# A four-layer network plus one block on one core: where the normed activations start in SBUF

## The reference

```
for i in range(4):                                   # mixers: retention, RG-LRU, MLA, retention
    h = layer_norm(ALPHA * h + mixer(h), ...)
    h = layer_norm(ALPHA * h + square(relu(h @ w1)) @ w2, ...)      # D_FF 4096
x = h + 0.5 * swiglu(rmsnorm(h), ...)                # D_FF 2816
x = x + hybrid_mixer(rmsnorm(x), ...)                # dilated attention + grouped-query attention, gated
x = x + 0.5 * swiglu(rmsnorm(x), ...)
return rmsnorm(x)
```

## The kernel before

| tensor | bytes after a slot's start, modulo 256 | used as |
|---|---|---|
| `ht_hi`, `ht_lo` | 64 | moving in U, stationary in T |
| `mlp_hi`, `mlp_lo` | 0 | stationary in D |
| `ffn_hi`, `ffn_lo` | 192 | stationary in D |
| `ry` (retention rows) | 64 | stationary in D |
| `lu` | 192 | stationary in D, moving in 60 U |
| `mo` of heads 0 to 3, of heads 4 to 7 | 160, 64 | stationary in D |
| `mrg` | 96 | stationary in D |
| `oa`, `ob`, `m_chi`, `m_clo` | 64 | moving in U |

## Time and profile before

### The profile page before, as it was taken

How to read it: one execution, slowest core, us unless ns; L and a number is a source line. 1 busy time by engine, 2 the same in 40 slices (tenths; PEclk the granted TensorE clock), 3 DMA queues, 4 the chain that set the end, 5 groups by cost and what they waited for, 6 DMA issues and landing times.

```text
span 2217.1 us, 31071 instructions
## 1 busy us (share of the span) xinstructions
PE 2089.2 (94%) x13232; PEld 1848.0 (83%) x13232; DVE 1284.3 (58%) x1205; ACT 924.5 (42%) x866; POOL 191.4 (9%) x76
## 2 busy tenths in 40 slices
PE   8999999978999879999999999989989999699998
PEld 7887899876998657998988799879978878687997
DVE  6756655687555635656656655564454556444544
ACT  5344333365333433333335433343344445444433
POOL 0001000121000113001000200010010003311000
PEclk9999999989999999999999999999999999999999
DMA  8443555434554404554544455525547543243552
GB/s 309 153 172 132 209 189 189 157 114 152 190 189 166 156 21 171 189 189 152 209 152 162 154 207 187 191 87 202 195 152 231 145 136 115 76 152 124 186 208 98
DMA packets 32366, 364.23 MB, mean 164 GB/s; under 512 B 3677, under 2 KB 3938, under 8 KB 10130
## 3 DMA queue, kind: packets, MB, share of 16 engines
q1 hardware_dynamic: 28146, 347.49, 42.6%
q0 software_dynamic: 4128, 15.39, 2.6%
HBM read 361.77 MB, written 1.10 MB: 164 GB/s over the span
## 4 chain that ended last, share of the span: by engine, by line
PE 84%; DVE 11%; ACT 3%; issue 1%; DMA 0%; SPq 0%; DVEq 0%; ACTq 0%
PE acc L860 25%; PE bank L820 15%; PE bank L822 14%; PE bank L821 14%; PE bank L847 2%; PE bank L849 2%; PE bank L848 2%; DVE h L2151 2%; PE bank L813 1%; PE bank L1372 1%; PE bank L1020 1%; PE bank L930 1%; PE bank L1408 1%; DVE w_lo L2078 1%; DVE h L2138 1%
## 5 line engine op out<-in xcount | busy, mean ns | idle before, releaser
L820 PE MATMUL bank<-ht_hi,w_hi 128*128 128x256 f32 x2720 | 764.8, 281 | 7.5 <-DVE ob_lo L2661 6.6
L822 PE MATMUL bank<-ht_hi,w_lo 128*128 128x256 f32 x2720 | 761.0, 280 | 0.0
L821 PE MATMUL bank<-ht_lo,w_hi 128*128 128x256 f32 x2720 | 760.2, 279 | 0.0
L820 PEld LDWEIGHTS bank<-ht_hi,w_hi 128*128 128x128 f32 x2720 | 511.4, 188 | 14.8 <-issue 12.7
L821 PEld LDWEIGHTS bank<-ht_lo,w_hi 128*128 128x128 f32 x2720 | 511.4, 188 | 2.5 <-issue 0.5
L822 PEld LDWEIGHTS bank<-ht_hi,w_lo 128*128 128x128 f32 x2720 | 512.5, 188 | 0.0
L2078 DVE TENSOR_TENSOR w_lo<-raw,w_hi 128x4096 fp32r<-128x4096 f32 (+3 forms) x87 | 328.0, 3770 | 142.7 <-ACT w_hi L1525 142.7
L1513 ACT ACTIVATE w_hi<-raw 128x2048 fp32r<-128x2048 f32 x174 | 323.4, 1908 | 143.4 <-PE bank L822 138.6
L1525 ACT ACTIVATE w_hi<-raw 128x4096 fp32r<-128x4096 f32 (+3 forms) x87 | 269.2, 3094 | 188.4 <-PE bank L822 188.4
L2073 DVE TENSOR_TENSOR w_lo<-raw,w_hi 128x2048 fp32r<-128x2048 f32 x98 | 220.2, 2288 | 113.3 <-ACT w_hi L1513 113.2
L789 POOL TENSOR_TENSOR w_lo<-raw,w_hi 128x2048 fp32r<-128x2048 f32 x18 | 82.4, 4579 | 1597.5 <-ACT w_hi L1513 1597.5
(11 more groups left out here) (321 smaller groups left out, 2726.0 us busy)
## 6 DMA issues: line engine op xcount, KB each, us to landing
raw<-slabs_in SPq DMA_DIRECT2D x147, 2048.0 KB, 7.7
raw<-slabs_in SPq DMA_DIRECT2D x23, 1024.0 KB, 6.3
raw<-slabs_in SPq DMA_DIRECT2D x12, 512.0 KB, 9.6
g_tab<-gains_in POOLq DMA_DIRECT2D x11, 512.0 KB, 6.7
a_bias<-bias_rows POOLq DMA_DIRECT2D x8, 576.0 KB, 6.9
b_tab<-gains_in POOLq DMA_DIRECT2D x8, 512.0 KB, 7.8
raw<-slabs_in SPq DMA_DIRECT2D x2, 1152.0 KB, 5.6
raw<-slabs_in SPq DMA_DIRECT2D x1, 1280.0 KB, 7.2
```

Source lines behind the costliest of these rows:

```text
L820: nc.tensor.matmul(o, whi, xhi, start=first, stop=False)
L821: nc.tensor.matmul(o, whi, xlo, start=False, stop=False)
L822: return nc.tensor.matmul(o, wlo, xhi, start=False, stop=last)
```

## The change

`ht_hi` and `ht_lo` get buffers that are 256 bytes longer. Inside them, each stage uses a view that begins `a` bytes in, with its own `a` for hi and for lo. The buffers themselves now begin at distance 0 from the slots, and `off_w` behind them is 256 bytes, so that everything behind moves by 512 bytes and keeps its distance modulo 256. `a` is thus the distance that the table above gives as 64 before:

| stage n | kind | `ht_hi`, `ht_lo` now | U of `ht` | T of `ht` |
|---|---|---|---|---|
| 0 | retention | 128, 128 | 768 | 192 |
| 1 | MLP | 128, 128 | 768 | |
| 2 | RG-LRU | 192, 192 | 480 | |
| 3 | MLP | 192, 192 | 768 | |
| 4 | MLA | 0, 0 | | 48, and 48 with 192 columns |
| 5 | MLP | 32, 32 | 768 | |
| 6 | retention | 64, 64 | 768 | 192 |
| 7 | MLP | 96, 96 | 768 | |
| 8 | FFN | 64, 192 | 1056 | |
| 9 | hybrid | 128, 0 | 960 | 288 |
| 10 | FFN | 160, 160 | 1056 | |

The three passes of U run in the order hi x hi, hi weights x lo activations, lo weights x hi activations; in stage 6 the last two change places.

```diff
+HT_PLACE = [(128, 128), (128, 128), (192, 192), (192, 192), (0, 0), (32, 32), (64, 64), (96, 96), (64, 192), (128, 0), (160, 160)]
+PASS_ORDER = [('whh', 'whl', 'wlh'), ('whh', 'whl', 'wlh'), ('whh', 'whl', 'wlh'), ('whh', 'whl', 'wlh'), ('whh', 'whl', 'wlh'), ('whh', 'whl', 'wlh'), ('whh', 'wlh', 'whl'), ('whh', 'whl', 'wlh'), ('whh', 'whl', 'wlh'), ('whh', 'whl', 'wlh'), ('whh', 'whl', 'wlh')]
...
-        off_w(64)
-        ht_hi = sb("ht_hi", [P, KD, S], F32R)
-        ht_lo = sb("ht_lo", [P, KD, S], F32R)
-        off_w(192)
+        ht_hi_buf = sb("ht_hi", [P, KD * S + 64], F32R)
+        ht_lo_buf = sb("ht_lo", [P, KD * S + 64], F32R)
+        ht_hi_at = [ht_hi_buf[:, a // 4:a // 4 + KD * S].rearrange("p (k s) -> p k s", k=KD) for a, _ in HT_PLACE]
+        ht_lo_at = [ht_lo_buf[:, a // 4:a // 4 + KD * S].rearrange("p (k s) -> p k s", k=KD) for _, a in HT_PLACE]
+        off_w(256)
...
-                nc.tensor.matmul(o, whi, xhi, start=first, stop=False)
-                nc.tensor.matmul(o, whi, xlo, start=False, stop=False)
-                return nc.tensor.matmul(o, wlo, xhi, start=False, stop=last)
+                passes = {"whh": (whi, xhi), "whl": (whi, xlo), "wlh": (wlo, xhi)}
+                for i, name in enumerate(order):
+                    w, x = passes[name]
+                    m = nc.tensor.matmul(o, w, x, start=first and i == 0, stop=last and i == 2)
+                return m
...
             for layer in range(DEPTH):
+                use_ht(2 * layer)
                 (retention, lru, mla)[layer % 3](layer)
+                use_ht(2 * layer + 1)
                 mlp(layer)
+            use_ht(N_LN)
             ffn(0)
+            use_ht(N_LN + 1)
             hybrid()
+            use_ht(N_LN + 2)
             ffn(1)
```

More of the change, by code:

```diff
@@ L799, in _, with use_ht @@
         def _(pe):
-            down_count = [0]
+            ht_hi, ht_lo, order = ht_hi_at[0], ht_lo_at[0], PASS_ORDER[0]
+            def use_ht(n):
+                nonlocal ht_hi, ht_lo, order
+                ht_hi, ht_lo, order = ht_hi_at[n], ht_lo_at[n], PASS_ORDER[n]
             def wait_free(*key):
@@ L1554, in ht_parts @@
                         act.wait_ge(*full(*key))
-                        nc.scalar.activation(ht_hi[:, 4 * half:4 * half + 4, t * P:(t + 1) * P],
+                        nc.scalar.activation(ht_hi_at[n][:, 4 * half:4 * half + 4, t * P:(t + 1) * P],
                                              psum(*key)[:, :].rearrange("p (c q) -> p c q", c=4), ACT.Copy)\
@@ L2098, in ht_part @@
                 dve.wait_ge(ht_hi_ready, 4 * n + 2 * t + half + 1)
-                nc.vector.tensor_tensor(ht_lo[:, c, q], psum(*key)[:, :].rearrange("p (c q) -> p c q", c=4),
-                                        ht_hi[:, c, q].bitcast(F32), ALU.subtract).then_inc(read_sem(*key), 1)
+                nc.vector.tensor_tensor(ht_lo_at[n][:, c, q], psum(*key)[:, :].rearrange("p (c q) -> p c q", c=4),
+                                        ht_hi_at[n][:, c, q].bitcast(F32), ALU.subtract).then_inc(read_sem(*key), 1)
             def ht_parts(n, tiles=range(TT)):
```

## The result

| | before | changed |
|---|---|---|
| median of 18 runs, us | 2220.97 | 2225.45 |
| ratio, 95% interval | | 1.0023 (1.0016 to 1.0029) |
| span of the profiled execution, us | 2217.1 | 2222.8 |

The account below looks back on a forecast made before the run. PE bounds the kernel, through the pitch of its U matmuls. From 2218.9 us, U adds 12.1 and T takes 0.6, swapped passes and other engines 0: 2230 us, stated median 2231; range 2199 to 2255, 8 in 10.

Parts of the forecast that it names:

- What bounds the kernel: PE, 84% of the chain of waits; U's 117.8 ns pitch goes into the time in full, clock unchanged.
- That the distance matters: D and T pitches differ by up to 6.6 ns with the stationary-minus-moving distance: good around 0, bad from 64 to 160.
- The second rival: Nothing changes: D's spread has another cause and U stays at 117.8 ns; 2219 to 2223 us, chance 15%.
- D's differences carried over to U at half size: U's change per matmul is (D(s - m) - 229.2) / 2, from -0.85 to +2.45 ns by stage; sum +12.1 us.
- sign of being wrong: For U: the prediction is wrong if places 96 to 192 are not slower than 64.
- the two distances without a row: D's unmeasured distances: 128 got its neighbours' mean, 233.9 ns; 224, between 192 and 0, got 228.4.
- the range from 2199 to 2255: Total time, us: holds the forecast, second rival, half the first and most of the third; 8 in 10.
- T and D by distance: T takes D's pitch at its new distance, stage 4 falling to 227.5 ns; T sum -0.6 us, D groups unchanged.
- The swapped passes: Stage 6: each pass reads at the same distance in either order, so 0 us; U stays at 117.8 ns.
- The first rival: U's fast 113.3 ns rhythm takes over: gain 16 us if half the changed stages, 30 if all; chance 27%.
- The third rival: A slower U rhythm: one 4.4 ns step gives +25 us, 2244 to 2247; chance 15%, 4 for over 2%.

Follow-up runs that it names:

- All-0: Changed kernel with ht_hi and ht_lo at place 0 in all 11 stages, passes in the old order: 2229.82 us, 1.0042 of before.
- all-224: Changed kernel with ht_hi and ht_lo at place 224 in all 11 stages, passes in the old order: 2226.66 us, 1.0028 of before.
- all-192: Changed kernel with ht_hi and ht_lo at place 192 in all 11 stages, passes in the old order: 2201.20 us, 0.9915 of before.

## Why the prediction was right, and which steps were not

**What bounds the kernel: right.** The pitch went into the time. By the pitches read, U should have added 4.9 us (below) and T taken 0.5; the span grew by 5.7, so about 1.3 us lie between the groups and are not assigned. The clock stayed, 0.977 against 0.978.

**That the distance matters: right.** All-0, all-224 and all-192 have the same instructions and differ by up to 28.6 us, while the shift by 96 bytes with equal distances is worth 0.06%, with an interval that holds no change. The second rival is refuted, and so is what the prediction drew from the Trainium skill, page "TensorE: Matmul & The Clock Gate", section "Step-by-step: what each phase is for": that the change would be worth nothing. Whether it is the two read ports that meet, no run shows.

**D's differences carried over to U at half size: the step that failed.** The prediction named a sign of being wrong that came true: U at place 192 was not slower than at 64, but faster (stage 2) or equal (stage 3). The rule gave the right sign of the total because it was near at 128 and 96, the places of three stages.

| stage, place | forecast ns | measured ns | us forecast | us measured |
|---|---|---|---|---|
| 0, 128 | 120.1 | 118.7 and 120.0 | +1.8 | +1.2 |
| 1, 128 | 120.1 | 120.0 (first 192: 118.7) | +1.8 | +1.5 |
| 2, 192 | 119.8 | 113.3 | +1.0 | -2.1 |
| 3, 192 | 119.8 | 117.8 (first 192: 113.3) | +1.6 | 0 |
| 5, 32 | 117.4 | 116.7 | -0.3 | -0.9 |
| 7, 96 | 120.0 | 120.0 | +1.7 | +1.7 |
| 8, 64 and 192 | 118.5 | 117.0 (first 192: 117.8) | +0.7 | -0.7 |
| 9, 128 and 0 | 119.1 | 120.0 (119.7 with the groups of 48) | +1.2 | +3.5 |
| 10, 160 | 120.2 | 118.7 (first 192: 117.3) | +2.6 | +0.7 |

The measured column is the number of U by the difference of pitches, stage by stage, and sums to +4.9 where the table summed to +12.1. Three errors lie in it. First, exchanging the roles of the operands doesn't carry over: place 0 was forecast a little better than 64 and is among the worst (all-0); 192, forecast worse, is the best (all-192). Second, stage 9: 384 of its U had run at 113.3, and I counted that loss nowhere in the sum: 384 x 6.7 = 2.6 us of its 3.5. Third, the two distances without a row were guessed from their neighbours, and 224 was guessed wrong: 228.4 ns, where T in all-224 has 233.3. With the true value the rule would have given stage 5 (place 32, distance 224) +2.05 ns a U, +1.6 us; it measured -0.9.

So the total owes something to luck. Stages 2, 3, 8 and 10 came out 8.0 us below their forecast, and the uncounted loss of stage 9 gave 2.6 back; without it the change would have cost about 2 us of U. The right sign at place 32 rests on a wrong guess. And the range from 2199 to 2255 was wide enough for almost any of this.

**T and D by distance: right where a row stood behind it.** 0 gives 226.7 in T as in D of `mlp`, 192 gives 228.9 in most T (all-192) as in D of `ffn` and, moved there, `ry`. Within one role a price could be carried from tensor to tensor. The limits: the guess for 224, above; 192 has a second rhythm at 233.3, in T and in D; and in stage 9, where the T pass with `ht_lo` was to gain 5.8 ns at place 0, all three passes stayed at 232.6 to 233.3, since a pair of unequal places is not the mean of its two. T came to -0.5 us all the same, 0.6 forecast.

**The swapped passes: right** for stage 6, 117.8 ns before and after; at 192 no new pitch either.

**The first rival** was true as a mechanism and not for these places: in this change only stage 2 and the entry of stage 3 had 113.3. It took place 192 in all stages to bring it to retention and FFN, and the gain was 19 us, between its 16 for half the stages and its 30 for all. Even there it doesn't always last: with the passes swapped, 480 U of the second retention stage and the whole first FFN were at 117.8. What the rival did not foresee is that D's place decides whether the rhythm lasts. **The third rival**: the slowest pitch seen in any run is 120.0; a step over that never came.

## What to carry to other kernels

Where back-to-back float32r matmuls fill the time, read the pitch from start to start, per group, before trusting any mean duration; a difference of 2 to 7 ns shows there exactly, while total times hide it under stages that cancel. If pitches differ between tensors of one shape, sweep the distance between stationary and moving operand, one value for the whole program at a time: a value per stage mixes the place with what the group before leaves behind. Carry a measured price from tensor to tensor in the same role, not across roles and not to a distance without a row, and judge a place also by whether the next group keeps its rhythm.

## What the runs showed of the hardware

- At a granted clock of 1.00, the 2.4 GHz level, steady pitches of U over 72 and more matmuls go from 113.33 to 120.00 ns, 272 to 288 cycles, with 116.67, 117.78, 118.33, 118.7 and 119.2 between. Those of D and T go from 226.67 to 234.2: 544 to 562 cycles. What unit sets the steps, and which reads meet in it, no run shows.
- U by place (ns, steady): 0 120.0; 16 118.7; 32 116.7, once 117.8; 48 118.3; 64 117.8 or 113.3; 96 120.0; 128 118.7 or 120.0; 160 118.7; 176 119.2; 192 117.8 or 113.3; 208 119.2; 224 118.3. That 256 bytes is the period was assumed; no run moves an operand by 256 alone.
- T and D by the stationary operand's place: 0 226.7; 64 233.3; 96 234.2; 128 232.2 to 232.5, in one T group of four 233.3; 192 228.9 or 233.3; 224 233.3.
- Either rhythm at 192 can hold for 480 U in a row, and through all the groups of a loop if its D operands lie at 192 too; behind D at 0 the U are slow in every loop. With `mlp` and `ht` at 192 the runs of one program spread by 9 to 20 us. With one rhythm throughout they spread by 1.3 (all-0) and 3.4 us (all-224).
